# Four edits to a fused two-block transformer kernel: halves of y, order of odd heads, a first slab in three passes, and six weight remainders computed by GpSimd

## What is computed

```python
u = h @ w_in                                   # one projection, cut into z, xbc, dt, q, k, v, gates
xbc = silu(centred_depthwise_conv(xbc, conv_w, conv_b))
y = y_f + y_b + d_skip[:, None] * xh           # both directions of the state-space scan
y = y.reshape(bsz, s, D_INNER) * silu(z)       # the state-space gate z
yg = y.reshape(bsz, s, 4, 512)
yg = yg * rsqrt(mean(square(yg), -1) + eps)    # a norm over each of 4 groups
```

## Time and profile before

| | |
|---|---|
| median of 3 runs | 1504.74 us (1504.03 to 1506.44) |
| the profiled execution's own time | 1504.41 us |
| its span, first to last instruction | 1502.6 us |
| mean granted TensorE clock | 0.985 |
| TensorE matmul busy | 1425.3 us (95%) |
| VectorE busy | 800.4 us (53%) |
| ScalarE busy | 551.8 us (37%) |
| GpSimd busy | 58.0 us (4%) |

### The profile page before, as it was taken

One profiled execution on the slowest core, in us unless ns is written; L12 is line 12 of the kernel. 1 busy time (PEld: TensorE's weight loads), 2 busy tenths in 40 slices (PEclk: granted clock), 3 DMA queues, 4 the chain that ended last, 5 costly groups with the idle time before them and its releaser, 6 DMA issues. The chain is left out here.

```text
span 1502.6 us, 20186 instructions
## 1 busy us (share of the span) xinstructions
PE 1425.3 (95%) x8684; PEld 1064.0 (71%) x8684; DVE 800.4 (53%) x1105; ACT 551.8 (37%) x701; POOL 58.0 (4%) x79
## 2 busy tenths in 40 slices
PE   6999999999988999999999979999988899999997
PEld 6987785443437788874434349899967799799886
DVE  4645552221227657551222254699899955655545
ACT  3344442111013354421101024588656553344432
POOL 1000000000003000000000010100111100000000
PEclk9999999999999999999999999999998999999999
DMA  8553686999994540389999974533411144445451
GB/s 342 176 215 114 252 334 265 429 427 427 429 426 165 175 162 1 113 314 416 427 427 428 428 331 165 210 113 123 159 57 57 57 168 169 177 154 202 170 194 58
DMA packets 27745, 355.16 MB, mean 236 GB/s; under 512 B 2881, under 2 KB 4929, under 8 KB 5761
## 3 DMA queue, kind: packets, MB, share of 16 engines
q1 hardware_dynamic: 25840, 341.85, 57.4%
q0 software_dynamic: 1808, 11.93, 2.1%
HBM read 352.72 MB, written 1.05 MB: 235 GB/s over the span
## 5 line engine op out<-in xcount | busy, mean ns | idle before, releaser
L2105 DVE TENSOR_TENSOR ring_low<-ring,w_rounded 128x2048 fp32r<-128x2048 f32 (+1 forms) x124 | 290.5, 2347 | 244.2 <-ACT w_rounded L1639 236.1
L1639 ACT ACTIVATE w_rounded<-ring 128x2048 fp32r<-128x2048 f32 (+1 forms) x124 | 235.2, 1899 | 311.7 <-PE ps L854 97.4
L854 PE MATMUL ps<-split,w_rounded 128*128 128x256 f32 x960 | 228.9, 286 | 17.5 <-DVE ring_low L2105 16.5
L854 PE MATMUL ps<-split,ring_low 128*128 128x256 f32 x736 | 209.7, 285 | 0.0
L854 PEld LDWEIGHTS ps<-split,w_rounded 128*128 128x128 f32 x960 | 168.7, 193 | 18.7 <-issue 16.2
L854 PE MATMUL ps<-hT_low,w_rounded 128*128 128x256 f32 x512 | 145.3, 284 | 0.0
L854 PEld LDWEIGHTS ps<-split,ring_low 128*128 128x128 f32 x736 | 141.2, 192 | 0.0
L884 PE MATMUL ps<-w_rounded,split 128*128 128x512 f32 (+1 forms) x352 | 124.5, 394 | 2.9 <-DVE split L2926 1.5
L2398 DVE TENSOR_SCALAR split<-ps,work 128x1024 fp32r<-128x1024 f32 x14 | 18.0, 1284 | 198.2 <-PE ps L1154 198.2
L1122 PE MATMUL ps<-work 128*64 128x512 f32 x448 | 100.9, 597 | 4.5 <-DMA work<-experts_w 4.5
L884 PE MATMUL ps<-ring_low,split 128*128 128x512 f32 (+1 forms) x256 | 99.0, 387 | 0.0
(11 more groups left out here) (368 smaller groups left out, 2438.3 us busy)
## 6 DMA issues: line engine op xcount, KB each, us to landing
ring<-slabs SPq DMA_DIRECT2D x65, 2048.0 KB, 8.1
work<-experts_w SPq DMA_DIRECT2D x48, 2048.0 KB, 20.7
ring<-experts_w SPq DMA_DIRECT2D x36, 2048.0 KB, 16.9
w_plain<-experts_w SPq DMA_DIRECT2D x12, 2048.0 KB, 16.7
gb<-ln_gb POOLq DMA_DIRECT2D x6, 1024.0 KB, 8.8
ring<-slabs SPq DMA_DIRECT2D x2, 1024.0 KB, 8.7
hT<-x_feat SPq DMA_DIRECT2D x1, 1024.0 KB, 5.0
work<-c_ret POOLq DMA_DIRECT2D x1, 1024.0 KB, 11.9
```

Of the source, the lines that this page charges most:

```text
L854: last = nc.tensor.matmul(dst[:, at:at + T], w3[a][:, k, c * P:(c + 1) * P], src[b][:, k, :], start=(k == 0 and t == 0), stop=(k == KC - 1 ...
L1639: nc.scalar.activation(rounded_half(q), half_of(ring, q), ACT.Copy).then_inc(w_high, 1)
L2105: V.tensor_tensor(half_of(ring_low, q), half_of(ring, q), rounded_half(q).bitcast(F32), ALU.subtract).then_inc(w_low, 1)
```

## The change

**Halves of y.** `take_y(g, 0)` now signals `y_half_out`. The diagonals at the first step of a group wait for that alone, and those of the third step for the other half. **Odd heads.** After an odd head TensorE runs `xbc_half` ahead of `att_products`, and VectorE `att_out` behind `conv`. **First slab.** Half 0 is multiplied pass by pass: pass 1 waits for the rounded weights and activations, pass 2 for the rest of the activations, pass 3 for the remainder of the weights. GpSimd waits for slab 2 before it issues the loads of `call`, `h` and `gb`. **Six remainders.** Remainders 2 to 7 of the state-space stage leave VectorE's program; GpSimd computes them behind the `xdt` of the last step of a group (remainder 2 behind step 3, 3 and 4 behind step 7, 5 and 6 behind step 11, 7 behind step 15), ahead of `root`.

```diff
             pool.dma_start(cret, c_ret).then_inc(stage_loaded, 16)
+            pool.wait_ge(slab_loaded[2], 16)
             pool.dma_start(call[:], c_all).then_inc(call_loaded, 16)
...
                 last.then_inc(xdt_ready, 1)
+                if c == 3:
+                    for q in range(HQ["ssd"] + max(2 * g + 1, 2), HQ["ssd"] + min(2 * g + 3, 8)):
+                        pool.wait_ge(w_high, q + 1)
+                        pool.wait_ge(w_low, q)
+                        nc.gpsimd.tensor_tensor(half_of(ring_low, q), half_of(ring, q), rounded_half(q).bitcast(F32),
+                                                ALU.subtract).then_inc(w_low, 1)
                 if c == 3 and g:
                     root(g - 1)
...
+            def start_half(dst):
+
+                pe.wait_ge(x_high, 1)
+                pe.wait_ge(w_high, 1)
+                w3 = split_weights(0, KC)
+                for n in range(3):
+                    if n == 1:
+                        pe.wait_ge(x_low, 1)
+                    elif n == 2:
+                        pe.wait_ge(w_low, 1)
+                    for c in range(2):
+                        for k in range(KC):
+                            last = nc.tensor.matmul(dst[:, c * T:(c + 1) * T], w3[n // 2][:, k, c * P:(c + 1) * P],
+                                                    r_hT[n % 2][:, k, :], start=(n == c == k == 0),
+                                                    stop=(n == 2 and c == 1 and k == KC - 1))
+                last.then_inc(half_done, 1)
...
-            pe.wait_ge(x_low, 1)
-            split_slabs("ret_in", 8, r_hT)
+            first_pair = take_pair(PJ["ret_in"])
+            start_half(first_pair)
+            split_columns(first_pair, 1, r_hT)
+            split_slabs("ret_in", 8, r_hT, 1)
...
-                att_products(hd)
-                xbc_half(hd + 2)
+                if hd % 2:
+                    xbc_half(hd + 2)
+                    att_products(hd)
+                else:
+                    att_products(hd)
+                    xbc_half(hd + 2)
...
-                dst = (take_pair(j) if c == 0 else pair(j))[:, c * T:(c + 1) * T]
+                dst = (take_pair(j) if p == 0 else pair(j))[:, c * T:(c + 1) * T]
+                if c == 0 and g:
+                    pe.wait_ge(y_half_out, g)
+                if c == 2 and g:
+                    wait_pair_out(pe, j - 2)
...
                 att_largest(hd + 2)
-                att_out(hd)
+                if hd % 2 == 0:
+                    att_out(hd)
                 low(HQ["att"] + hd + 3)
                 conv(hd)
+                if hd % 2:
+                    att_out(hd)
...
-                    link(last)
+                    last.then_inc(y_half_out, 1)
+                    dve.wait_ge(y_half_out, g + 1)
...
                     gate_y(g - 1)
-                    low(HQ["ssd"] + (p + 2) // 2)
...
-                if c == 1:
-                    low(HQ["ssd"] + (p + 3) // 2)
+                if p == 13:
+                    dve.wait_ge(w_low, HQ["ssd"] + 8)
+                    low(HQ["ssd"] + 8)
```

More of the change, by code:

```diff
@@ L444, in build @@
         ssd_y_ready, square_ready = sem("ssd_y_ready"), sem("square_ready")
+        y_half_out = sem("y_half_out")
         root_ready, root_diag_ready, y_low = sem("root_ready"), sem("root_diag_ready"), sem("y_low")
```

## The result

The changed kernel takes 1511.06 us in the median of 15 runs (1508.01 to 1515.54), the kernel before beside it 1507.19 (1504.03 to 1509.00): a ratio of 1.0029, with an interval of 1.0018 to 1.0039, slower by 0.29% or about 4.4 us (the two medians themselves lie 3.9 apart). The forecast was 1505.8, no change; the time lies inside the range of 1498 to 1513, on the side that had a chance of 0.32. Of the 5.3 us between 1505.8 and 1511.06, 2.5 lie in the kernel before itself, whose median was 1504.74 over three runs and is 1507.19 over fifteen; the change is to be read against +1.4, and it is about 3 us worse than that. The profiled execution of the changed kernel took 1508.03 us, 3.6 more than that of the kernel before, and its span is 1506.2.

The account below looks back on a forecast made before the run. VectorE was taken to bound the second block's attention and the state-space stage, TensorE or expert loads the rest. First slab -1.4, odd heads -1.6, halves of y 0, remainders +4.4 made +1.4 on 1504.41: 1505.8 us, range 1498 to 1513.

Parts of the forecast that it names:

- the side that had a chance of 0.32: Whole program: slower than the kernel before by more than the 3.0 us that a measurement can tell; chance 0.32.
- the 6.51: Recorded us of an earlier GpSimd subtraction of the same shape, read as 2.03 waiting for VectorE's remainder, then 4.48 running.
- the fourth: Start and attention: three passes and odd heads win nothing, remainders still cost 4.4, so 1508.8 us, slower; chance 0.09.
- Rival 1: State-space stage: GpSimd's remainder takes longer than 4.43 us; 1510.4 at 5.2, 1518 at 6.51, slower; chance 0.23.
- rival 2: State-space stage: GpSimd's reads fit between VectorE's, the block is small; 1486.6 us, or 1498.1 with 40%, faster; chance 0.14.
- rival 3: State-space group: TensorE sets the pace and halves of y pay, -10.3 us more, 1495.5, faster; chance 0.09.

Follow-up runs that it names:

- mended kernel: Changed kernel with VectorE's cret wait behind half slab 2's remainder, each GpSimd remainder in eight instructions, root between a group's two remainders: 1498.40 us, ratio 0.9955.

## Where the prediction held and where it failed

| term | forecast | measured | by |
|---|---|---|---|
| first slab | -1.4 | about 0 | half 2 left at 33.1 with it, 33.0 without |
| odd heads | -1.6 | -0.55 | four pairs 0.12 longer, 1 us at the end |
| halves of y | 0 | +0.2 | 126.28 against 126.07 |
| remainder 2 | -0.6 | -1.25, -0.92, -0.94 | clamps, three kernels; up to 1.1 of doubt |
| remainder 3 | +2.2 | +2.15, +2.22 | clamps, two kernels |
| remainder 4 | +0.4 | +0.63, +0.63, +0.63 | clamps |
| remainder 5 | +1.0 | +1.08, +1.01 | clamps |
| remainder 6 | +0.4 | +0.63, +0.65, +0.65 | clamps |
| remainder 7 | +1.0 | +1.03, +1.00 | clamps |
| sum | +1.4 | +4.0 | |

The measured sum takes 4.3 for the remainders, as in the changed kernel; it goes with the +3.6 of the two profiled executions and with the 4.4 of the ratio. Of the 2.6 us between the sums the first slab has 1.4 and the odd heads 1.05.

**The six remainders** came out as worked out in their mechanism: +4.3 for +4.4, remainders 3, 5 and 7 within 0.1 us each. That the sums agree so closely is partly luck. Remainders 4 and 6 cost 0.23 more each than forecast and remainder 2 less, and the -0.6 of remainder 2 doesn't follow from its own numbers: 1.6 won (1113.08 to 1111.5) less two blocks of 0.6 leaves -0.4. A state-space group takes 32.6 us after (1129.21 to 1161.80) where the prediction named 31 to 32. The two questions that the prediction put, how long and what it stops, were the right ones. How long: 4.55 to 4.60 us where GpSimd starts with nothing in its way, against 4.43 taken. The Trainium skill (GPSIMD Engine Reference, 3.1 Elementwise — side-by-side cycle accounting) has 4497 ns for an addition; these rows are 0.05 to 0.1 above that, and the 4.43 from VectorE's stretched row is 0.12 to 0.17 below them. The 5.23 at 1122.37 is the same instruction waiting out the end of gate_y, as the prediction read the 6.51. What it stops: gate_y and the products, as forecast. Missing was that root_diagonal is stopped too, by the xdt that follow root: 1.14 us for its two rows at 1139.99, where it takes 0.48 in the last group, with no xdt beside it; the 0.98 in the earlier trace rows had been so stretched before, so the change adds 0.16.

**The first slab** is the step that failed first: "TensorE begins half 2 at about 26.3 instead of 27.7". The 26.3 held (26.57). The 27.7 was the wrong thing to set against it. It is one execution's, and in the other kernels without the edit half 2 is left up to 0.9 us earlier; TensorE gets through the first halves sooner in these and comes to the same floor, the landing of cret and 2.29 us of remainder. The prediction named that floor as what is late next, and then priced the edit at the distance from it in one trace. Why TensorE gets through its first products at different speeds is open: from 16 to 19 us the profile before has 16 of them and the one with the remainders alone 22, both at a granted clock of 1.00. That the clock can be down behind the gap, as in one of the four profiles, was not thought of.

**The odd heads** failed in one sentence: "att_out behind conv in odd heads moves 0.29 us of VectorE and adds none". An instruction moved on the engine that sets the pace moves what it frees: the bank is free later, the even head's products wait for it, and VectorE waits 0.2 us for a rounding that comes later. The waits are in the trace, and the pair grows by 0.12 us with VectorE's order alone; that the one wait brings the other is argued from their order. The other half, that only VectorE's own waits can be won, held: TensorE lost its 3.9 us of waits and nothing came of it. Of the 1.6 us forecast at the end about 1 was won; one wait of 1.00 us is left there.

**Halves of y** came out at nothing, for the reason given: TensorE's waits in the stage are slack, and the 10.3 us came back as other waits.

Of the rivals, the fourth (first slab and odd heads win nothing, 1508.8) is nearly what the profiled execution shows, 1508.03; it had 0.09. Its reason for the slab isn't what happened, since cret lands no later with the edit (VectorE's remainder starts behind it at 24.2 to 24.4, and at 23.95 to 24.8 without). It should still have had more: both small terms were read off single waits in one trace and taken at nearly their full size, while the one large term was built from durations. Rival 1 asks for over 4.75 us of GpSimd, rival 2 for no block, rival 3 for a TensorE that sets the pace; none of them is so.

## What to carry to other kernels

Where two engines can't run certain instructions at once, as GpSimd's remainders and VectorE's products here, handing work from one to the other can cost more than it frees, and what counts is how long one instruction blocks, not the sum of the work. The same six remainders cost 4.3 us in one piece each and 1.1 in eight pieces; in eight pieces and with root between them the stage is 5.6 us shorter than before. When an instruction is put ahead of a short one that others wait for, as ahead of root, the short one goes first. And when a start is made earlier, find the landing that the next step waits for, and move that wait in the same edit.

## What the hardware showed beside

**The granted clock at one place differs from run to run.** The kernel before, the one with the even remainders and the one with the halves of y issue the same work up to the state-space stage. The stretch from 215 to 260 us, around the first router, in these three profiles:

```profile
215.00:260.00 45.00, 43.85 (x247) 28.65 (x246) 17.28 (x42) 13.45 (x23) 0.63 (x1) 0.96 0.68 262
```

```profile
215.00:260.00 45.00, 42.96 (x252) 27.45 (x252) 16.50 (x41) 14.00 (x26) 0.63 (x1) 1.00 0.71 276
```

```profile
215.00:260.00 45.00, 44.24 (x227) 28.86 (x225) 16.92 (x41) 12.98 (x23) 0.63 (x1) 0.89 0.63 238
```

The granted clock is 0.96, 1.00 and 0.89 of 2.4 GHz, so a part of the stretch ran at 1.2 GHz in two of them. TensorE's first wait for the router there, 0.40 us, stands in all three, also where the clock stayed up; why it fell in one execution and not in another is not shown. From the end of this wait to the products behind the router (line 977 in the kernel before) it takes 13.3, 12.7 and 16.1 us, so the two profiles with a lower clock are 0.6 and 3.4 us longer at this place. The stage begins at 1088.60, 1089.02 and 1091.24: the 3.4 us are in part still there (with a granted clock of 0.97 from 640 to 700 besides), the 0.6 are not. The profile with the remainders alone had 0.89 here, 0.91 from 640 to 700, and began the stage at 1094.20; it lost 2.6 more at its end, behind the seventh place. There its clock was 0.87, before 1.00, and in the changed kernel 0.88:

```profile
1201.26:1227.50 26.24, 23.29 (x181) 20.61 (x180) 19.55 (x36) 13.86 (x13) 0.69 (x1) 0.87 0.23 81
```

```profile
1191.08:1214.67 23.59, 21.85 (x194) 19.74 (x192) 19.66 (x36) 13.93 (x13) 0.69 (x1) 1.00 0.26 90
```

```profile
1194.33:1217.95 23.62, 22.65 (x176) 19.95 (x176) 18.95 (x36) 12.99 (x13) 0.69 (x1) 0.88 0.25 90
```

The changed kernel lost nothing by the same mean clock. Its lower level lay from 1194.33 to 1198 (0.50), while VectorE had its clamps and products to do; with the remainders alone it lay around 1217 to 1221 (0.50), where VectorE waits for TensorE: 2.59 us instead of 1.71 ahead of it, and 2.12 instead of 0.31 behind it. So in these two profiles the low clock cost time where TensorE was what VectorE waited for, and none where it wasn't.

Differences of this size between executions are larger than three of the four edits. Two profiles are therefore set against each other between places that hold the same work, as the clamps here, and not from the start of the span. The mended kernel's profile, too, is of an execution of 1502.07, 3.7 above its median, with 0.89 in this stretch.

**VectorE's busy time holds the time for which it was stopped.** It fell by 0.5 us in the stage when 13.7 us of work went, since the stopped instruction's record runs on. The Trainium skill (SBUF — State Buffer, Who interferes with whom) tells of a lock held for a whole instruction; the eight pieces agree, with 2.52 us in place of 4.80 for the same pair of products.
